# Copying the diagonal blocks of a recurrence on VectorE instead of GpSimd, with one step of the schedule cut from 1.7 to 1.25 chunks

## The chip, the cores and the metric

The kernel runs on one core of one Trainium2 chip. The metric is the device time in microseconds of one launch; lower is better. Short names of the engines: PE is TensorE, DVE is VectorE, ACT is ScalarE, POOL is GpSimd, SP is SyncE (it issues the weight loads).

## The reference, cut to what matters

Two layers; in each, one input projection feeds three branches (stick-breaking attention, latent attention, an RWKV-7 recurrence), and gates merge them. The change touches only the recurrence:

```python
def step(state, inp):
    r_t, w_t, k_t, v_t, a_t, b_t = inp
    sa = jnp.einsum('bhij,bhj->bhi', state, a_t)
    state = (state * w_t[:, :, None, :] + sa[..., None] * b_t[:, :, None, :]
             + v_t[..., None] * k_t[:, :, None, :])
    return state, jnp.einsum('bhij,bhj->bhi', state, r_t)
```

## The kernel before, in words

**Dense work.** Every weight matrix is streamed through SBUF as 280 chunks per layer (two blocks of 128 rows, mostly 512 columns). SP loads a chunk into a ring, ACT rounds it to its high half (`w_hi`, line 1043), DVE subtracts to get the low half (`w_lo`, the "split", line 1416), and PE multiplies: a chunk is 12 matmuls, six per half chunk (line 724). A split of a full chunk is a 128x1024 subtraction.

**Everything else is woven in by hand.** Each engine runs one program in a fixed order. The small work is divided into beats; `STEPS` gives each beat's length in chunks, and `beat_at(n)` turns the n-th beat into a position in the stream of chunks: the cumulated lengths are scaled so that all of them together fill the chunks 50 to 208, and each position is rounded down to half a chunk. PE runs to `beat_at(n)` in half chunks; DVE, ACT and POOL run to `int(beat_at(n))`. When DVE stands at position k it has split chunk k+2 (`LEAD` is 3), so PE, which waits for the count of splits at the first half of each chunk, can run at most through chunk k+2.

**The recurrence.** Eight heads are taken in four pairs of heads ("pair 0" to "pair 3"), 19 beats each, with two beats of other work between pair 0 and pair 1. A pair begins so:

- PE, after the pair's first beat: the score matmuls (16 of 64x256, line 829 through the helper at line 724), then `beat(4)`, that is four beats of dense work, then the first of four levels (`G1`, four small matmuls that need `WT`), a beat, `G2`, a beat, and so on.
- DVE: four predicated copies of 128x512 from PSUM put the masked scores into `AM` (line 1547); `beat(2)`; then, once POOL has copied the diagonal blocks, a chain of small operations that inverts the 8x8 blocks (lines 1551 to 1569, each linked to the one before, with one extra split at m == 2: `dense_to(int(beat_at(beats[0])) + 1)`); `beat()`; the tail of the chain (lines 1571 to 1583), whose transposes at line 1579 make `WT` and whose last product makes `WA`; `beat()`.
- POOL: four copies of 32x128, one per quarter of the partitions, take the diagonal blocks out of `AM` into `UC` (line 587), then the mask of the first level (line 575) and two copies (line 593).

For a pair whose first beat is number b+1, the score matmuls stand at `beat_at(b+1)`, the DVE chain after `beat_at(b+3)`, its tail after `beat_at(b+4)`, and `G1` of the first level at `beat_at(b+5)`. In the kernel before these positions are:

| pair | scores | after `beat(2)` | before the tail | `G1`, first level |
|---|---|---|---|---|
| 0 | 50.5 | 52.5 | 54.0 | 57.0 |
| 1 | 73.5 | 75.5 | 77.0 | 80.0 |
| 2 | 92.5 | 94.5 | 96.0 | 99.0 |
| 3 | 111.5 | 113.5 | 115.0 | 117.5 |

ACT evicts a finished group of dense columns from PSUM when it passes the group's last chunk (gates at 64, 72, 80, 88, ... 120, then `uq0` 122, `ukv0` 124, `uq1` 126, `ukv1` 128, and the recurrence's own gate `rg` at 144). For `rg` DVE has work too: it multiplies, transposes (lines 1462, 1416, 1446), all at its position 144. The latent attention's preparation for its second pair of heads (line 1641 a reduction, a beat, line 1644 a second one, a beat, line 1653 four scalings, a beat) stands around that point.

Of the kernel before, what the change touches and what calls it, by code (L numbers as in the profile page):

```python
# [59 lines left out]
LEVELS = 4  # L60
LEVELS_IN = 3
# [94 lines left out]
AT_KK = AT_Z + 1  # L156
AT_DECAY = AT_KK + 9
AT_PAIRS = AT_DECAY + 5
RW_STEPS = [1, 1.2, 1, 1.7, 2.96] + [0.92, 1.02] * LEVELS + [0.88] * 6
LATENT_STEPS = [2, 2.5]  # L160
GN_STEPS = [0.9] * 8
ML_PREP, ML_VISITS = [1.1, 1.2, 1.3, 1.2, 1.4, 1.4], [2, 1.5, 1.4]
# [2 lines left out]
SB_STEPS = [4, 3.5, 3]  # L165
RW_BEATS, GN_BEATS, ML_BEATS, SB_BEATS = len(RW_STEPS), len(GN_STEPS), len(ML_STEPS), len(SB_STEPS)
STEPS = RW_STEPS + LATENT_STEPS + 3 * RW_STEPS + GN_STEPS + ML_STEPS + SBH // 2 * SB_STEPS
AT_STEP = [sum(STEPS[:n]) for n in range(len(STEPS) + 1)]
# [27 lines left out]
AT_RW, AT_ML1, AT_SB = END["mg1"] + 2, END["mg1"] + 4, END["br0"]  # L196


RW_PE, RW_ACT, RW_DVE, RW_POOL = 8 + 2 * LEVELS, 5 + LEVELS, 5 + 2 * LEVELS, 6 + LEVELS_IN


def level_ready(n):

    if n >= LEVELS_IN:
        return RW_POOL - LEVELS + n
    return 5 if n == 1 else 6 + n


def program(nc, x, norm_g, w_in, mla_q_norm_g, mla_kv_norm_g, mla_w_uq, mla_w_ukv, mla_qn_g, mla_kn_g,
# [3 lines left out]
    with ExitStack() as ctx:  # L213
# [6 lines left out]
        def one(name):  # L220
            return ctx.enter_context(nc.semaphore(name))
# [30 lines left out]
        def units(n, u):  # L252
            return take(n).rearrange("p (u c) -> p u c", u=u)
# [21 lines left out]
        UC, WC = units(128, 4), units(128, 4)  # L275
# [3 lines left out]
        AM = units(2048, 4)  # L279
# [94 lines left out]
        rw_pe, rw_act, rw_dve, rw_pool = one("rw_pe"), one("rw_act"), one("rw_dve"), one("rw_levels")  # L374
# [145 lines left out]
        def _(pool):  # L520
# [7 lines left out]
            for l in range(DEPTH):  # L528
# [41 lines left out]
                def beat(count=1):  # L570
                    beats[0] += count
                    dense_to(int(beat_at(beats[0])))

                def rw_level(p, n):
                    nc.gpsimd.tensor_tensor(LM.rearrange("p u (a c) -> p u a c", a=2),
                                            UC.unsqueeze(2).to_broadcast([P, 4, 2, 32]),
                                            level[n].rearrange("p (a c) -> p a c", a=2).unsqueeze(1)
                                            .to_broadcast([P, 4, 2, 32]), ALU.mult).then_inc(rw_pool, 1)

                for p in range(4):  # L580
                    if p == 1:
                        beat(len(LATENT_STEPS))
                    beat()
                    pool.wait_ge(rw_dve, 4 * RW_DVE * l + RW_DVE * p + 2)
                    for q in range(4):
                        r = slice(32 * q, 32 * q + 32)
                        nc.gpsimd.tensor_copy(UC[r, :, :], AM[r, :, r]).then_inc(rw_pool, 1)  # L587
                    pool.wait_ge(rw_pool, 4 * RW_POOL * l + RW_POOL * p + 4)
                    rw_level(p, 1)
                    pool.wait_ge(rw_pool, 4 * RW_POOL * l + RW_POOL * p + 5)  # L590
                    for a in range(2):
                        r = slice(64 * a, 64 * a + 32)
                        nc.gpsimd.tensor_copy(LM5[r, :, 32 * a:32 * a + 32], AM[r, :, 64 * a + 32:64 * a + 64]
                                              ).then_inc(rw_pool, 1)
                    beat(4)
                    pool.wait_ge(rw_pool, 4 * RW_POOL * l + RW_POOL * p + 7)
                    for n in range(1, LEVELS_IN - 1):
                        pool.wait_ge(rw_pe, 4 * RW_PE * l + RW_PE * p + 1 + 2 * n)
                        rw_level(p, n + 1)
                        beat(2)  # L600
                    pool.wait_ge(rw_pe, 4 * RW_PE * l + RW_PE * p + 2 * LEVELS_IN - 1)
                    nc.gpsimd.tensor_copy(LM, AM[:, :, 64:128]).then_inc(rw_pool, 1)
                    pool.wait_ge(rw_pool, 4 * RW_POOL * l + RW_POOL * p + RW_POOL)
                    if p < 3:
                        turned = OPS_TURN.rearrange("p h (i j t) -> p h i j t", i=4, j=4)
                        moved = TT2[(p + 1) % 2].rearrange("p h (i j t) -> p h i j t", i=4, j=4)
                        pool.wait_ge(ops_turned, 3 * l + p + 1)
                        for d in range(4):
                            for i in range(4):
                                j = (i + d) % 4  # L610
                                nc.gpsimd.tensor_copy(moved[32 * j:32 * j + 32, :, :, i, :],
                                                      turned[32 * i:32 * i + 32, :, :, j, :]).then_inc(quarters, 1)
                            pool.wait_ge(quarters, 16 * (3 * l + p) + 4 * d + 4)
                        pool.sem_inc(ops_moved, 1)
                    beat(6)
                    beat(6)
# [49 lines left out]
                for q in range(SBH // 2):  # L666
# [6 lines left out]
                    for e in range(2):  # L673
                        pool.wait_ge(sb_act, 8 * l + 4 * q + 3 + e)
                        for c0 in (0, 256):
                            part = AZ[e][:, c0:c0 + P]
                            last = nc.gpsimd.affine_select(out=part, in_=part, compare_op=ALU.is_gt, fill=0.0,
                                                           base=0, pattern=[[1, P]], channel_multiplier=-1)
# [41 lines left out]
        def _(pe):  # L720
# [26 lines left out]
            def dense_to(end):  # L747

                while at[0] < end:
                    n, kk = int(at[0]), round(at[0] % 1 * KC)  # L750
                    gi, c = CHUNKS[n]
                    name, _, _, cols, blocks = GROUPS[gi]
                    if kk == 0:
                        if c == 0 and gi >= 2:
# [284 lines left out]
        def _(act):  # L1039
# [27 lines left out]
            def take_out(end):  # L1067
                while group[0] < len(GROUPS) and END[GROUPS[group[0]][0]] <= end:
                    gi = group[0]
                    name, _, _, cols, blocks = GROUPS[gi]  # L1070
                    group[0] += 1
                    kind, no = name.rstrip("0123456789"), int(name[-1]) if name[-1].isdigit() else 0
# [332 lines left out]
        def _(dve):  # L1405
            v = nc.vector
            at, group, beats, order = [0], [GI["rg"]], [0], [0]

            def link(ins):

                order[0] += 1
                ins.then_inc(dve_seq, 1)
                dve.wait_ge(dve_seq, order[0])

            def tt(o, a, b, op):
                return v.tensor_tensor(o, a, b, op)  # L1416
# [18 lines left out]
            def beat(count=1):  # L1435
                for _ in range(count):
                    beats[0] += 1
                    dense_to(int(beat_at(beats[0])))
# [95 lines left out]
            def rw_pair(p):  # L1534
# [10 lines left out]
                    dve.wait_ge(rw_pool, 4 * RW_POOL * l + RW_POOL * p)  # L1545
                for u in range(4):
                    last = v.copy_predicated(AM[:, u, :], con[:, K_RWM:K_RWM + 512].bitcast(U32), B[u][:])  # L1547
                last.then_inc(rw_dve, 1)
                beat(2)
                dve.wait_ge(rw_pool, 4 * RW_POOL * l + RW_POOL * p + 4)  # L1550
                blocks = own_block.unsqueeze(1).unsqueeze(3).to_broadcast([P, 4, 32 // EDGE, EDGE])
                wide = WIDE[:, 0:128].rearrange("p (u j c) -> p u j c", u=4, j=32 // EDGE)
                link(tt(wide, UC.rearrange("p u (j c) -> p u j c", c=EDGE), blocks, ALU.mult))
# [7 lines left out]
                for m in range(1, EDGE - 1):  # L1561
                    n, c0 = EDGE - 1 - m, 32 - m
# [15 lines left out]
                for g in range(2):  # L1578
                    last = v.transpose(WT[64 * g:64 * g + 64, :, 32 * g:32 * g + 32], WC[64 * g:64 * g + 64, :, :])  # L1579
# [5 lines left out]
                for n in range(1, LEVELS_IN):  # L1585
                    beat()
                    dve.wait_ge(rw_pe, 4 * RW_PE * l + e + 2 * n + 2)
                    for g, (odd, rows) in product(range(2), PARITY):
                        half = slice(32 * g, 32 * g + 32)
                        t = WT[64 * g:64 * g + 64, odd, half]  # L1590
                        last = tt(t, t, G2[rows:rows + 64, odd, half], ALU.add)
                    last.then_inc(rw_dve, 1)
                    dve.wait_ge(rw_dve, 4 * RW_DVE * l + RW_DVE * p + 2 * n + 3)
                    for q in (1, 3) if n == LEVELS_IN - 1 else range(4):
                        r = slice(32 * q, 32 * q + 32)
                        last = v.transpose(WA[r, :, q % 2 * 32:q % 2 * 32 + 32], WT[r, :, q // 2 * 32:q // 2 * 32 + 32])
                    last.then_inc(rw_dve, 1)
                    if p < 3:
                        if n == 1 and p:
                            dve.wait_ge(ops_moved, 3 * l + p)  # L1600
                        for i in (2 * n - 2, 2 * n - 1):
                            s = (KK, R[:, :, 0:512], AA, R[:, :, 512:1024])[i]
                            last = v.transpose(OPS_TURN[:, :, i * P:(i + 1) * P], s[:, :, (p + 1) * P:(p + 2) * P])
                        if n == LEVELS_IN - 1:
                            last.then_inc(ops_turned, 1)
                    if n == LEVELS_IN - 1:
                        for q in range(4):
                            r = slice(32 * q, 32 * q + 32)
# [4 lines left out]
                for odd, rows in PARITY:  # L1613
                    last = v.transpose(WT6[32:64, odd, 0:32], G2[rows:rows + 32, odd, 0:32])
                last.then_inc(rw_dve, 1)
                for i, (odd, rows) in product(range(2), PARITY):
                    r = rows + 32 * i
                    last = v.tensor_copy(WF[64 * i:64 * i + 32, odd, 64 * i + 32:64 * i + 64], G2[r:r + 32, odd, 0:32])
# [3 lines left out]
                for odd, rows in PARITY:  # L1622
                    last = v.tensor_copy(WF[0:64, odd, 64:128], G2[rows:rows + 64, odd, :])
# [149 lines left out]
            for l in range(DEPTH):  # L1773
# [47 lines left out]
                for h in range(HALVES):  # L1821
                    last = v.scalar_tensor_tensor(S1[:, h, :], AA[:, h, :], -1.0, ROWS[:, 512:1024], ALU.add, ALU.mult)
                link(last)
                dense_to(AT_KK + 2)
                for h in range(HALVES):
                    last = v.scalar_tensor_tensor(R[:, h, 512:1024], S1[:, h, :], 1.0, R[:, h, 512:1024],
                                                  ALU.add, ALU.mult)
# [20 lines left out]
                for h in range(HALVES):  # L1848
                    last = v.scalar_tensor_tensor(KK[:, h, :], KK[:, h, :], -1.0, S3[:, h, :], ALU.mult, ALU.mult)
# [10 lines left out]
                for p in range(4):  # L1860
                    if p == 1:
                        latents()
                    rw_pair(p)
# [90 lines left out]
```

## Time and profile before

| | |
|---|---|
| runs | 1682.27, 1680.42, 1680.75 us; median 1680.75 us |
| profiled execution, its own time | 1682.79 us |
| its span, first to last instruction | 1681.0 us |
| PE busy / DVE / ACT / POOL | 1665.9 / 1154.5 / 841.7 / 489.8 us |
| TensorE clock granted | 1.00 of full speed throughout (the 2.4 GHz level) |
| HBM | 195 GB/s over the span |

How to read it: matmuls are pipelined and their ends are modelled, so "busy" of PE includes waits shorter than about the 0.16 us by which a matmul's shown 0.39 us exceeds the spacing of two matmuls. Waits of PE are therefore read here as distances between starts. In a timeline a row is start, duration, engine, line, operation, the tiles, the shapes, the count of merged instructions, and in brackets the idle time before it and who ended it. Lines are those of the kernel before.

### The profile page before, as it was taken

How to read it: one execution, taken by the hardware profiler on the slowest of the kernel's cores; microseconds unless marked ns; L12 is line 12 of the kernel's file. 1: busy time of each engine (PE TensorE's matmuls, PEld its weight loads, DVE VectorE, ACT ScalarE, POOL GpSimd, SP SyncE). 2: the span in 40 equal slices, each digit the busy share in tenths (PEclk: the TensorE clock that was granted, in tenths of full speed). 3: DMA queues.
4: the chain of work that ended last, by engine and by line, in shares of the span. 5: the costliest groups of instructions: out<-in, count | busy, mean ns of one | idle time of the engine just before them, and what ended most of it. 6: DMA issues, size and time to landing. Idle time of an engine off the chain costs nothing.

```text
span 1681.0 us, 21448 instructions
## 1 busy us (share of the span) xinstructions
PE 1665.9 (99%) x8010; PEld 1390.0 (83%) x8010; DVE 1154.5 (69%) x1667; ACT 841.7 (50%) x1221; POOL 489.8 (29%) x722
## 2 busy tenths in 40 slices
PE   7999999999999999999999999999999999999999
PEld 6878888888888888888888788888888888888887
DVE  4668775866976566886656786857778665578853
ACT  6544554435545455555454445534445544555542
POOL 1011313410343426362400112233103534245500
PEclk9999999999999999999999999999999999999999
DMA  8865656656665557785687656556566565668764
GB/s 260 262 179 184 185 166 189 183 159 189 180 183 172 176 163 235 234 307 188 207 264 229 180 175 178 187 163 200 162 180 181 168 177 177 187 211 289 262 193 158
DMA packets 176912, 332.72 MB, mean 198 GB/s; under 512 B 19516, under 2 KB 32746, under 8 KB 176808
## 3 DMA queue, kind: packets, MB, share of 16 engines
q1 hardware_dynamic: 167048, 297.86, 58.3%
q0 software_dynamic: 9584, 33.42, 5.7%
q8 instruction: 63, 1.03, 0.3%
q14 instruction: 41, 0.34, 0.1%
q10 hardware_dynamic: 176, 0.07, 0.0%
HBM read 311.14 MB, written 16.78 MB: 195 GB/s over the span
## 4 chain that ended last, share of the span: by engine, by line
PE 90%; DVE 4%; ACT 2%; DMA 1%; SPq 1%; issue 1%; POOL 1%; ACTq 0%; DVEq 0%
PE D L724 81%; PE B L724 8%; DMA ring<-in_w_in 1%; DVE w_lo L1416 1%; DVE arena L1416 1%; ACT w_hi L1043 1%; POOL arena L587 1%; ACT arena L1043 1%; DVE arena L1547 0%; PE B L915 0%; DVE xy L1416 0%; SPq L464 0%; ACT gev L1043 0%; PE B L894 0%; DVE ht_lo L1750 0%
## 5 line engine op out<-in xcount | busy, mean ns | idle before, releaser
L1416 DVE TENSOR_TENSOR w_lo<-ring,w_hi 128x1024 fp32r<-128x1024 f32 (+3 forms) x560 | 677.1, 1223 | 330.8 <-ACT w_hi L1043 321.9
L1043 ACT ACTIVATE w_hi<-ring 128x1024 fp32r<-128x1024 f32 (+3 forms) x560 | 575.0, 1038 | 486.1 <-PE D L724 379.4
L724 PE MATMUL D<-w_hi,ht_hi 128*128 128x512 f32 (+2 forms) x1728 | 680.7, 394 | 4.3 <-DVE w_lo L1416 4.1
L724 PE MATMUL D<-w_hi,ht_lo 128*128 128x512 f32 (+2 forms) x1728 | 665.5, 385 | 0.0
L724 PE MATMUL D<-w_lo,ht_hi 128*128 128x512 f32 (+2 forms) x1728 | 664.8, 385 | 0.0
L724 PEld LDWEIGHTS D<-w_hi,ht_hi 128*128 128x128 f32 x1728 | 325.0, 188 | 74.1 <-issue 8.8
L724 PEld LDWEIGHTS D<-w_hi,ht_lo 128*128 128x128 f32 x1728 | 324.6, 188 | 65.9
L724 PEld LDWEIGHTS D<-w_lo,ht_hi 128*128 128x128 f32 x1728 | 325.2, 188 | 58.9 <-issue 0.5
L626 POOL COPY arena<-arena 32x256 f32<-32x256 f32 x240 | 163.2, 680 | 144.6 <-DVE arena L1446 108.9
L724 PEld LDWEIGHTS B<-arena 128*128 128x128 f32 (+2 forms) x928 | 121.7, 190 | 20.8 <-issue 8.1
L1043 ACT ACTIVATE arena<-B 64x64 f32<-64x64 f32 (+6 forms) x186 | 54.9, 300 | 165.0 <-PE B L724 158.8
L643 POOL COPY arena<-arena 32x384 f32<-32x384 f32 x128 | 95.8, 748 | 135.3 <-PE B L724 103.1
L724 PE MATMUL B<-arena 128*128 128x128 f32 (+4 forms) x928 | 132.7, 295 | 1.7 <-DVE arena L1579 0.7
L724 PE MATMUL D<-w_hi,mt_lo 128*128 128x512 f32 x256 | 100.5, 392 | 0.0
L724 PE MATMUL D<-w_hi,mt_hi 128*128 128x512 f32 x256 | 100.3, 392 | 0.0
L724 PE MATMUL D<-w_lo,mt_hi 128*128 128x512 f32 x256 | 100.0, 390 | 0.0
L566 POOL DMA_DIRECT2D gate_spill<-gev x24 | 17.8, 742 | 251.9 <-ACT gev L1043 250.8
L1416 DVE TENSOR_TENSOR arena<-arena 128x1024 f32<-128x1024 f32 (+9 forms) x168 | 86.4, 514 | 5.1 <-DMA arena<-arena 0.3
L587 POOL COPY arena<-arena 32x128 f32<-32x128 f32 x32 | 24.0, 749 | 166.6 <-DVE arena L1547 165.2
L1043 ACT ACTIVATE arena<-arena 128x1024 f32<-128x1024 f32 (+5 forms) x88 | 58.9, 669 | 11.4 <-DVE arena L1416 7.8
L1043 ACT ACTIVATE gev<-D,small 128x512 f32<-128x512 f32 (+1 forms) x64 | 40.4, 680 | 35.5 <-PE D L724 35.3
L724 PEld LDWEIGHTS D<-w_lo,mt_hi 128*128 128x128 f32 x256 | 48.1, 188 | 10.7
(163 smaller groups left out, 1386.8 us busy)
## 6 DMA issues: line engine op xcount, KB each, us to landing
ring<-in_w_in SPq DMA_DIRECT2D x368, 512.0 KB, 4.5
ring<-in_w_out SPq DMA_DIRECT2D x64, 512.0 KB, 5.2
ring<-in_w_br_mla SPq DMA_DIRECT2D x32, 512.0 KB, 5.5
gate_spill<-gev POOLq DMA_DIRECT2D x24, 512.0 KB, 4.7
arena<-gate_spill POOLq DMA_DIRECT2D x24, 512.0 KB, 5.7
ring<-in_mla_w_ukv SPq DMA_DIRECT2D x16, 512.0 KB, 4.4
ring<-in_w_br_rw SPq DMA_DIRECT2D x16, 512.0 KB, 5.2
ring<-in_w_br_sb SPq DMA_DIRECT2D x16, 512.0 KB, 5.4
```

Source lines behind the costliest of these rows:

```text
L566: pool.dma_start(spill[n].rearrange("(h p) c -> p h c", p=P), gev[:, n % 2, :, :]).then_inc(spilled[n % 2][l], 16)
L587: nc.gpsimd.tensor_copy(UC[r, :, :], AM[r, :, r]).then_inc(rw_pool, 1)
L626: nc.gpsimd.tensor_copy(moved[32 * j:32 * j + 32, :, :, i, :], turned[32 * i:32 * i + 32, :, :, j, :]).then_inc(quadrants[l], 1)
L643: nc.gpsimd.tensor_copy(moved[32 * j:32 * j + 32, :, i, :], turned[32 * i:32 * i + 32, :, j, :]).then_inc(ml_quarters, 1)
L724: return nc.tensor.matmul(o, a, b, start=start, stop=stop, skip_group_check=True)
L1043: return nc.scalar.activation(o, i, fn, **kw)
L1416: return v.tensor_tensor(o, a, b, op)
```

## The change

DVE makes the four 32x128 copies right behind its predicated copies, linked to the last of them; POOL no longer makes them and starts with the first level's mask. POOL's count of signals per pair drops by four. DVE's later wait is on its own copies. The length of the step behind the masked scores is 1.25 instead of 1.7 chunks for each of the four pairs of each layer; since all lengths are scaled to the same 158 chunks, every other step grows by 1%, and positions move by up to one chunk.

```diff
-RW_STEPS = [1, 1.2, 1, 1.7, 2.96] + [0.92, 1.02] * LEVELS + [0.88] * 6
+RW_STEPS = [1, 1.2, 1, 1.25, 2.96] + [0.92, 1.02] * LEVELS + [0.88] * 6
...
-RW_PE, RW_ACT, RW_DVE, RW_POOL = 8 + 2 * LEVELS, 5 + LEVELS, 5 + 2 * LEVELS, 6 + LEVELS_IN
+RW_PE, RW_ACT, RW_DVE, RW_POOL = 8 + 2 * LEVELS, 5 + LEVELS, 5 + 2 * LEVELS, 2 + LEVELS_IN
...
-    return 5 if n == 1 else 6 + n
+    return 1 if n == 1 else 2 + n
...
                     pool.wait_ge(rw_dve, 4 * RW_DVE * l + RW_DVE * p + 2)
-                    for q in range(4):
-                        r = slice(32 * q, 32 * q + 32)
-                        nc.gpsimd.tensor_copy(UC[r, :, :], AM[r, :, r]).then_inc(rw_pool, 1)
-                    pool.wait_ge(rw_pool, 4 * RW_POOL * l + RW_POOL * p + 4)
                     rw_level(p, 1)
-                    pool.wait_ge(rw_pool, 4 * RW_POOL * l + RW_POOL * p + 5)
+                    pool.wait_ge(rw_pool, 4 * RW_POOL * l + RW_POOL * p + 1)
...
                     last = v.copy_predicated(AM[:, u, :], con[:, K_RWM:K_RWM + 512].bitcast(U32), B[u][:])
+                link(last)
+                for q in range(4):
+                    r = slice(32 * q, 32 * q + 32)
+                    last = v.tensor_copy(UC[r, :, :], AM[r, :, r])
                 last.then_inc(rw_dve, 1)
                 beat(2)
-                dve.wait_ge(rw_pool, 4 * RW_POOL * l + RW_POOL * p + 4)
+                dve.wait_ge(rw_dve, 4 * RW_DVE * l + RW_DVE * p + 2)
```

## Rows read from the trace of the kernel before

**Rows 1.** The page, busy time of an engine, its share and instructions:

```profile
PE 1665.9 (99%) x8010; PEld 1390.0 (83%) x8010; DVE 1154.5 (69%) x1667; ACT 841.7 (50%) x1221; POOL 489.8 (29%) x722
```

**Rows 2.** Waits: engine, line, releaser, us in total, times, longest:

```profile
DVE arena L1416 <- POOL arena L587: 7.4, 8, 1.2
```

**Rows 3.** Timeline of DVE, layer 0, pair 1:

```profile
229.42 2.61 DVE L1547 COPY_PREDICATED arena<-con,B 128x512 f32<-128x512 uint32 x4 [2.54 <-PE B L724]
231.92 2.44 DVE L1416 TENSOR_TENSOR w_lo<-ring,w_hi 128x1024 fp32r<-128x1024 f32 x2
235.24 0.29 DVE L1416 TENSOR_TENSOR arena<-arena,con 128x128 f32<-128x128 f32 x1 [0.88 <-POOL arena L587]
...
242.78 1.22 DVE L1416 TENSOR_TENSOR w_lo<-ring,w_hi 128x1024 fp32r<-128x1024 f32 x1
243.93 0.65 DVE L1416 TENSOR_TENSOR arena<-arena,con 128x256 f32<-128x256 f32 x1
...
245.40 0.62 DVE L1579 STREAM_TRANSPOSE arena<-arena 64x128 f32<-64x128 f32 x2
...
246.40 3.49 DVE L1416 TENSOR_TENSOR w_lo<-ring,w_hi 128x1024 fp32r<-128x1024 f32 x3
```

**Rows 4.** Timeline of PE, layer 0, pair 1:

```profile
229.31 0.50 PE L724 MATMUL D<-w_hi,ht_hi 128*128 128x512 f32 x1
...
244.44 0.39 PE L724 MATMUL D<-w_hi,ht_hi 128*128 128x512 f32 x1
...
245.80 0.39 PE L724 MATMUL D<-w_hi,ht_hi 128*128 128x512 f32 x1
...
247.16 0.61 PE L724 MATMUL B<-arena 128*128 128x128 f32 x4
247.76 0.47 PE L724 MATMUL D<-w_hi,ht_hi 128*128 128x512 f32 x1
...
249.56 0.68 PE L724 MATMUL B<-arena 128*128 128x128 f32 x4 [0.17 <-ACT arena L1043]
```

**Rows 5.** Timeline of PE, layer 0, pair 3:

```profile
354.87 0.50 PE L724 MATMUL D<-w_hi,ht_hi 128*128 128x512 f32 x1
...
371.88 0.71 PE L724 MATMUL B<-arena 128*128 128x128 f32 x4 [0.34 <-DVE arena L1579]
...
381.28 0.61 PE L724 MATMUL B<-arena 128*128 128x128 f32 x4
...
383.28 0.71 PE L724 MATMUL B<-arena 128*128 128x128 f32 x4 [0.32 <-DVE arena L1416]
...
392.31 0.61 PE L724 MATMUL B<-arena 128*128 128x128 f32 x4
392.68 0.42 PE L724 MATMUL D<-w_hi,cq_hi 128*128 128x384 f32 x1
...
393.81 0.55 PE L724 MATMUL B<-arena 128*128 128x64 f32 x4
```

**Rows 6.** Timeline of ACT, layer 0, pair 1 at the first level:

```profile
247.36 1.27 ACT L1043 ACTIVATE gev<-D,small 128x512 f32<-128x512 f32 x2 [1.60 <-PE D L724]
```

**Rows 7.** One line's instructions (ns min/median/max), the nearest copy in SBUF:

```profile
L1845 DVE COPY arena<-arena x2: 226/226/227, 133.6 to 965.1; 128x128 f32<-128x128 f32 x2
```

**Rows 8.** Timeline of POOL, layer 0, pair 1:

```profile
232.10 3.10 POOL L587 COPY arena<-arena 32x128 f32<-32x128 f32 x4 [6.40 <-DVE arena L1547]
235.29 0.84 POOL L575 TENSOR_TENSOR arena<-arena,con 128x256 f32<-128x256 f32 x1
```

**Rows 9.** Timeline of DVE, layer 0, behind the gate at chunk 144:

```profile
454.92 0.64 DVE L1644 TENSOR_REDUCE small<-arena 128x4 f32<-128x512 f32 x1
...
455.70 1.21 DVE L1416 TENSOR_TENSOR w_lo<-ring,w_hi 128x1024 fp32r<-128x1024 f32 x1
456.84 1.64 DVE L1653 SCALAR_TENSOR_TENSOR arena<-arena,small 128x192 f32<-128x192 f32 x4
```

**Rows 10.** Timeline of PE, layer 0, the same place, chunk 147:

```profile
456.97 0.50 PE L724 MATMUL D<-w_hi,ht_hi 128*128 128x512 f32 x1 [0.43 <-DVE w_lo L1416]
```

More of the change, by code:

```diff
@@ L595, in _ @@
                     beat(4)
-                    pool.wait_ge(rw_pool, 4 * RW_POOL * l + RW_POOL * p + 7)
+                    pool.wait_ge(rw_pool, 4 * RW_POOL * l + RW_POOL * p + 3)
                     for n in range(1, LEVELS_IN - 1):
```

## The prediction

> **What bounds the kernel now.** I read the page's busy times first: PE is busy 99% of the span [rows 1], so no work elsewhere counts unless PE waits for it. Then the table of waits: DVE waited for POOL's diagonal copies eight times, once per pair and layer, for 7.4 us in all [rows 2]; the largest thing the change can take away is therefore idle time of an engine that is not the bound. Then the timelines of PE and DVE side by side, pair by pair, because the busy share hides short waits: there the distances between starts are compared. They show that PE does lose time in the recurrence, in small pieces. All times below are in pair 1's clock of layer 0; pair 0 repeats it 75 us earlier, and layer 1 repeats layer 0.
>
> **What PE loses before.** Twelve matmuls from 244.44 to 247.16 [rows 4] give 0.227 us each. The first level's `G1` of pair 1 is followed by dense work after 0.60 us [rows 4], where a `G1` without a wait takes 0.37 [rows 5]: 0.24, because the split of the next chunk, the first of the three at 246.40 [rows 3], ends only then. Pair 0 does the same. The half chunk behind it takes 1.80 us to `G2` [rows 4], six matmuls being 1.36 plus about 0.1 at the restart: about 0.35, as ACT was evicting a gate, 1.27 us from 247.36 [rows 6], before it could copy `G1`'s result. Pair 3 needs 17.01 us for the 72 matmuls from 354.87 to 371.88 [rows 5], which pair 1 does from 229.31 to 245.80, 16.49 us [rows 4]: 0.52, and about 0.1 within the `G1` that waits for line 1579. At its third level the way from `G2` to `G1` takes 2.00 us, against 1.50 for the same six narrower matmuls later [rows 5]: 0.5 and another 0.1. The sum is 0.48 + 0.35 + 0.62 + 0.6 = 2.05 per layer, with a tenth or two in pairs 0 and 2 about 2.4: **4.8 us in two layers is all that the change can win.** By the same reading of starts the rest of the program has little to give.
>
> **The copies.** DVE's predicated copies run from 229.42 to 232.03, the two splits behind them start at 231.92, and the chain starts at 235.24 after 0.88 us of waiting for POOL [rows 3]. After: a link (about 0.03), four copies, then the same two splits, then the chain without a wait. The nearest copy in SBUF with 128 elements per partition took 0.226 us [rows 7], four of them 0.90; with a gap I take 0.92. The splits then start about 1.0 to 1.1 us later than before, and the 0.88 us goes: **the chain starts 0.12 us later, not earlier.** The wait was hidden behind the splits, and the copies are not. Bounds, as estimates around that row: 0.17 each (a quarter under it, for a quarter of its partitions) to 0.30 (a third over it, for a strided source), so the chain starts between 0.1 earlier and 0.45 later.
>
> A rule speaks here: the Trainium skill, VectorE: DVE Perf Modes, section "The TRN2 errata — SBUF-src ops pay a fixed extra latency per instruction", gives 58 cycles plus elements over the mode's speed-up at 0.96 GHz, that is an estimated 0.13 us for 128 elements at double speed, but notes that a fixed term near 150 cycles was measured, which gives 0.22. The row's 0.226 us agrees with the second [rows 7]; by the first the copies would cost 0.4 us less per pair, and the time would come out about 3.3 us lower, at 1683.3 us.
>
> **The step.** The lengths sum to 172.7 instead of 174.5, scaled to the same 158 chunks. Rounded down to half chunks, the positions after are:
>
> | pair | scores | after `beat(2)` | before the tail | `G1` |
> |---|---|---|---|---|
> | 0 | 50.5 | 52.5 | 54.0 | 56.5 |
> | 1 | 73.5 | 75.5 | 76.5 | 79.5 |
> | 2 | 92.0 | 94.0 | 95.5 | 98.0 |
> | 3 | 111.0 | 113.0 | 114.0 | 117.0 |
>
> Between scores and `G1` PE now has 6.0 chunks in every pair (6.5, 6.5, 6.5, 6.0 before). DVE takes the integer part, and m == 2 already takes it one chunk past `beat(2)`: in pairs 1 to 3 the step before the tail brings no split any more (76, 95, 114 are reached at m == 2), so `WT` comes 243.93 - 242.78 = 1.15 us earlier [rows 3] less the 0.12, and that split now follows the tail. What PE may do before the tail is over is chunk k+2.
>
> - Pair 0 keeps its split at 54. `WT` is ready at 245.40 + 0.62 + 0.12, with a handoff of 0.06 at 246.20; PE arrives half a chunk earlier, at 245.80 [rows 3, 4]. New wait **0.45**; the wait behind `G1` goes.
> - Pair 1: DVE stands at 76 and PE may run through chunk 78, but `G1` stands at 79.5 and needs the first half of chunk 79. PE asks for it at 244.44 [rows 4]. Its split, which ended just before that in the kernel before (242.78 + 1.22 [rows 3]), now follows the tail: the tail and `WA` take 246.40 - 243.93 = 2.47 us [rows 3], so the split starts at 242.78 + 0.12 + 2.47 = 245.37, ends at 246.59, and PE goes on some 0.14 later, as it did after the first of the three splits before. New wait **2.3**. Behind PE's wait for this chunk stand `G1`, and so ACT's copy and DVE's next additions. The half chunk before `G2` stays, but the gate's eviction moves behind ACT's copy, so that 0.35 goes.
> - Pairs 2 and 3: DVE stands at 95 and 114, enough for exactly the six chunks. `G1` starts at 245.80 without waiting, but the next dense chunk, asked for 0.37 later, waits for the first split behind the tail until 246.73: **0.57** each. The losses of pair 3 named above go.
> - In pair 3 the gate of chunk 120 is now evicted between `G2` of the second and `G1` of the third level, with narrow chunks behind it. ACT's 1.27 us [rows 6] comes ahead of two small copies that `G2` needs; I put **0.3**, between nothing and 0.5.
>
> New waits per layer: 0.45 + 2.3 + 0.57 + 0.57 + 0.3 = 4.2, or 8.4 in all, for the 4.8 that go.
>
> **Behind the recurrence** the latent attention stands up to a chunk earlier. At the gate `rg` (chunk 144) DVE's position 144 moves one beat back, behind line 1644, and position 145 behind line 1653. PE asked for chunk 147 just when its split ended: it waited 0.43 [rows 10] for the split at 455.70 [rows 9]. After, the scalings of line 1653 (1.64 us [rows 9]) stand ahead of that split and the reduction of line 1644 with its addition (0.78, from 454.92 to 455.70 [rows 9]) no longer: 0.8 later, and some 0.3 because ACT's work on the first squares now delays its sigmoids. **1.1 per layer**, 2.2 in all, bounds 0 and 1.6 each.
>
> **Sum.** 8.4 + 2.2 - 4.8 = +5.8 us on the profiled execution's span of 1681.0 (its own time is 1682.79, some 2 us above the median, of which 1.79 lie outside the span and are not touched). On the median: 1680.75 + 5.8, **1686.5 us**.
>
> **Rivals.**
> 1. *Not slower: the copies cost nothing.* If DVE stands idle before the splits anyhow (waiting for ACT's high half), the copies fill that time and the chain starts 0.88 earlier. Then pair 0, 2 and 3 have no new wait and pair 1 has 1.3: with 0.3 that is 3.2 in two layers, less 4.8, and with the gate's order harmless 1679.2 us. It decides when the chain starts 0.6 or more earlier. Against it: 231.92 follows 232.03 without a gap [rows 3]. For it: that row is pair 1's, and another pair's splits may wait for ACT.
> 2. *Within the bound: only the recurrence changes.* The gate at 144 and ACT at 120 cost nothing: 1680.75 + 7.8 - 4.8 = 1683.7 us. For it: the 0.43 there is one layer's [rows 10], the order of three engines decides it, and I have no row of the new order.
> 3. *Worse: POOL gets in ahead of the splits.* POOL's first mask, 0.84 us [rows 8], is now released by the same event behind which the splits start. Before, POOL's four copies took 3.10 us because the splits were ahead of them [rows 8]; if POOL starts first and the split is held until it is done, every pair's chain is 0.84 later: 4 x 0.84 x 2 = 6.7, 1693.2 us. Against it: the splits need no signal, POOL does. The Trainium skill, SBUF — State Buffer, section "SBUF: two separate sides", states that the pair of ports shared by the two engines is locked for a whole instruction by whoever starts first; POOL's 3.10 us agrees with that, in the order DVE first.
>
> **Chances.** Forecast 0.73, rival 1 0.07, rival 2 0.15, rival 3 0.05. A difference of 0.2%, 3.4 us, is about what a measurement of this kernel tells from none. Slower (above 1684.1): the forecast less the part of its bounds below that, and rival 3, 0.76. Within: rival 2, most of rival 1 and that part, 0.20. Faster: 0.04, since even all 4.8 us without any new wait would be only 0.29%. Range: the copies' bounds move four waits in two layers by -1.9 to +2.4, the gate -2.2 to +1.0, ACT -0.6 to +0.4; 1682.5 to 1690.0 holds 8 in 10.
>
> **What would show it.** Right: PE waits about 2 us for a `w_lo` split in pair 1 of both layers ahead of `G1`, the largest wait in the table of PE; DVE's wait for POOL is gone, yet its chain starts about 5.9 us after the first predicated copy instead of 5.8 [rows 3]; pair 3's waits for lines 1579 and 1416 are gone. Wrong: no wait of PE over 1 us in pair 1 (then the order of split and tail is not as I read it), a chain that starts over 0.5 us earlier, or copies of more than 0.3 us each. The gate at 144 shows in PE's wait for chunk 147, 1 to 2 us.

## The result, and the profile after

The changed kernel takes **1693.49 us**, median of 5 runs (1691.10 to 1696.42), against 1680.75: a ratio of 1.0075, 95% interval 1.0063 to 1.0086. It is slower, as forecast, but by 12.7 us where 5.8 were forecast, and outside the range of 1682.5 to 1690.0.

Its profiled execution took 1691.10 us with a span of 1689.3, 8.3 more than before's. The page, busy time of an engine, its share and instructions (answers [rows 1]):

```profile
PE 1666.2 (99%) x8010; PEld 1389.6 (82%) x8010; DVE 1165.1 (69%) x1699; ACT 843.4 (50%) x1221; POOL 477.7 (28%) x690
```

PE does the same work in the same busy time; the 8.3 us are waits. The table of waits for PE (engine, line, releaser, total us, times, longest); the row of [rows 2], DVE waiting for POOL, has no counterpart any more:

```profile
PE D L720 <- DVE w_lo L1412: 12.5, 15, 2.6
```

The timeline of DVE in pair 1 of layer 0 (answers [rows 3]; lines 589 to 1543 of the kernel after are 593 to 1547 of before, and each experiment's lines are its own kernel's):

```profile
228.17 2.60 DVE L1543 COPY_PREDICATED arena<-con,B 128x512 f32<-128x512 uint32 x4 [2.54 <-PE B L720]
230.80 0.91 DVE L1547 COPY arena<-arena 32x128 f32<-32x128 f32 x4
231.74 2.91 DVE L1412 TENSOR_TENSOR w_lo<-ring,w_hi 128x1024 fp32r<-128x1024 f32 x2
234.58 0.37 DVE L1412 TENSOR_TENSOR arena<-arena,con 128x128 f32<-128x128 f32 x1
...
243.68 0.62 DVE L1579 STREAM_TRANSPOSE arena<-arena 64x128 f32<-64x128 f32 x2
...
244.68 3.49 DVE L1412 TENSOR_TENSOR w_lo<-ring,w_hi 128x1024 fp32r<-128x1024 f32 x3
```

The same from 233.3 us on, which leaves the second of the two splits alone in its row:

```profile
232.89 1.77 DVE L1412 TENSOR_TENSOR w_lo<-ring,w_hi 128x1024 fp32r<-128x1024 f32 x1
```

And POOL's timeline there (answers [rows 8]):

```profile
231.80 1.77 POOL L575 TENSOR_TENSOR arena<-arena,con 128x256 f32<-128x256 f32 x1 [7.36 <-DVE arena L1547]
233.63 1.51 POOL L589 COPY arena<-arena 32x128 f32<-32x128 f32 x2
```

The copies cost what was forecast, 0.91 us. But the two splits behind them take 2.91 us instead of 2.44: the first runs its usual time, the second 1.77 us instead of 1.2. POOL's mask starts with the first split, lasts 1.77 us instead of 0.84, and ends 0.68 us after the second split began. So the chain starts 6.41 us after the first predicated copy (228.17 to 234.58), where before's took 5.82: **0.59 later instead of 0.12**. Between the chain and its tail no split stands any more, and three follow the tail at 244.68.

In pair 3 the chain is as late (6.39 us after the first predicated copy), but there another wait decides. ACT evicts a gate ahead of the high half that the second split needs (ACT's and DVE's timelines of pair 3):

```profile
358.49 1.27 ACT L1039 ACTIVATE gev<-D,small 128x512 f32<-128x512 f32 x2 [3.80 <-PE D L720]
```

```profile
359.07 1.23 DVE L1412 TENSOR_TENSOR w_lo<-ring,w_hi 128x1024 fp32r<-128x1024 f32 x1
360.74 1.24 DVE L1412 TENSOR_TENSOR w_lo<-ring,w_hi 128x1024 fp32r<-128x1024 f32 x1 [0.44 <-ACT w_hi L1039]
```

PE's timeline in layer 0: pair 1 (answers [rows 4]), pair 2, pair 3 (answers [rows 5]), and the gate (answers [rows 10]):

```profile
242.96 0.39 PE L720 MATMUL D<-w_hi,ht_lo 128*128 128x512 f32 x1
245.95 0.50 PE L720 MATMUL D<-w_hi,ht_hi 128*128 128x512 f32 x1 [2.61 <-DVE w_lo L1412]
...
308.46 0.61 PE L720 MATMUL B<-arena 128*128 128x128 f32 x4
309.87 0.50 PE L720 MATMUL D<-w_hi,ht_hi 128*128 128x512 f32 x1 [0.81 <-DVE w_lo L1412]
...
371.89 0.60 PE L720 MATMUL B<-arena 128*128 128x128 f32 x4
373.30 0.50 PE L720 MATMUL D<-w_hi,ht_hi 128*128 128x512 f32 x1 [0.80 <-DVE w_lo L1412]
...
385.93 0.63 PE L720 MATMUL B<-arena 128*128 128x64 f32 x4 [0.16 <-ACT arena L1039]
...
460.14 0.50 PE L720 MATMUL D<-w_hi,ht_hi 128*128 128x512 f32 x1 [1.01 <-DVE w_lo L1412]
```

By distances between starts, as in the prediction: pair 1 loses 2.99 - 0.23 = 2.77 us, pairs 2 and 3 1.41 - 0.37 = 1.05 each, pair 0 0.46 and 0.47 for two waits of 0.29, pair 3's ACT copies 0.33. That is 6.1 per layer. At the gate the wait grows from 0.43 [rows 10] to 1.01; layer 1, where before's trace shows no such wait, loses 1.17. Together 12.2 + 0.6 + 1.2 = 14.0 us of new waits.

What went in return can be read as well, since PE runs the same 6722 matmuls of dense work in the same order in both kernels. The start of the same one in both:

| the same dense matmul | before | after | later by |
|---|---|---|---|
| layer 0, ahead of pair 0's first level | 159.17 | 157.07 | -2.10 |
| layer 0, behind the four pairs | 449.57 | 452.16 | 2.59 |
| layer 0, behind the gate | 678.28 | 681.48 | 3.20 |
| layer 1, ahead of pair 0's first level | 997.44 | 1000.41 | 2.97 |
| layer 1, behind the four pairs | 1283.11 | 1290.58 | 7.47 |
| layer 1, behind the gate | 1514.75 | 1523.07 | 8.32 |

The four pairs cost 4.7 and 4.5 us net and the gates 0.6 and 0.85: **10.7 us**. So of the 12.2 us of new waits in the pairs only 3.0 were won back. Profile to profile it is 8.3, since before's profiled execution is 2.1 us behind ahead of the first pair, in the opening, where the change alters nothing.

The other four runs of the kernel after lie 2.1 to 5.3 us above the profiled one, with a mean granted clock of 0.998 or 0.999 where the profiled one has 1.000. This profile can't show what took them; the experiments do.

### The profile page after: what moved, and what is told of

Same layout as the page of the kernel before. It is cut to its first block, busy times and chain, and to the rows that moved or that the text cites. A ratio compares the mean times of both kernels' runs of the same rounds, so it can differ in the third digit from the quotient of the medians.

```text
span 1689.3 us, 21442 instructions
## 1 busy us (share of the span) xinstructions
PE 1666.2 (99%) x8010; PEld 1389.6 (82%) x8010; DVE 1165.1 (69%) x1699; ACT 843.4 (50%) x1221; POOL 477.7 (28%) x690
## 4 chain that ended last, share of the span: by engine, by line
PE 85%; DVE 9%; ACT 2%; DMA 1%; issue 1%; SPq 1%; ACTq 0%; DVEq 0%
PE D L720 76%; PE B L720 8%; DVE w_lo L1412 3%; DVE arena L1412 3%; DMA ring<-in_w_in 1%; DVE arena L1543 1%; ACT w_hi L1039 1%; ACT arena L1039 0%; ACT gev L1039 0%; DVE xy L1412 0%; DVE arena L1547 0%; PE B L911 0%; DVE arena L1579 0%; DVE gev L1458 0%; SPq L449 0%
## 5 line engine op out<-in xcount | busy, mean ns | idle before, releaser
L720 PE MATMUL D<-w_hi,ht_hi 128*128 128x512 f32 (+2 forms) x1728 | 681.0, 394 | 12.7 <-DVE w_lo L1412 12.5
L622 POOL COPY arena<-arena 32x256 f32<-32x256 f32 x240 | 167.5, 698 | 143.6 <-DVE arena L1442 107.9
L639 POOL COPY arena<-arena 32x384 f32<-32x384 f32 x128 | 90.4, 707 | 134.1 <-PE B L720 83.8
L575 POOL TENSOR_TENSOR arena<-arena,con 128x256 f32<-128x256 f32 x16 | 22.9, 1430 | 249.4 <-DVE arena L1547 174.5
L720 PEld LDWEIGHTS D<-w_hi,mt_lo 128*128 128x128 f32 x256 | 48.1, 188 | 11.2
```

What stands on the lines that cost most here:

```text
L639: nc.gpsimd.tensor_copy(moved[32 * j:32 * j + 32, :, i, :], turned[32 * i:32 * i + 32, :, j, :]).then_inc(ml_quarters, 1)
L720: return nc.tensor.matmul(o, a, b, start=start, stop=stop, skip_group_check=True)
```

## The experiments

Each time is a median, beside runs of before on the same chip, with medians of 1681.0 to 1681.3; the intervals are of the ratio to before, and the clocks are each run's mean.

**The two parts apart.** First the copies on DVE with the step back at 1.7:

```diff
-RW_STEPS = [1, 1.2, 1, 1.25, 2.96] + ...
+RW_STEPS = [1, 1.2, 1, 1.7, 2.96] + ...
```

> After, with the step behind the masked scores back at 1.7 chunks: the copies on VectorE alone. Late-split theory (most of the loss comes from TensorE coming sooner than the split that stands behind the chain): no wait near 2.7 us in pair 1; the chain starts 0.6 us later than in before because the two splits beside POOL's mask still take 2.9 us, which adds at most 0.6 us to each of the waits that before has in pairs 1 and 3 and as much at new places, 1 to 2 us a layer: 1682.5 to 1685, granted clock 1.000 in every run. Rival (the copies on VectorE with the contention beside them are the cause): 1689 to 1693.

Measured 1685.64 us, 1.0028 (1.0017 to 1.0038), clock 1.000 in all 8 runs. So the copies alone cost 4.5 us, just above what the theory gave. The chain starts 6.41 us after the first predicated copy here too, and in layer 0 PE loses 0.3 to 0.6 us by starts at nine places from the first pair to the gate, where before's profile has four.

Then before with the step at 1.25, POOL still copying (the same edit the other way):

> Before, with the step behind the masked scores at 1.25 chunks: POOL still copies the blocks. Late-split theory: the chain starts 5.8 us after the first predicated copy, as in before, and the waits of after stay less 0.6 us each: pair 1 about 2.2 us, pairs 2 and 3 about 0.45, pair 0 next to nothing, the gate 1.2: 2.5 us a layer less than after's profiled 1691.1, so 1686, up to 1688 if the clock falls in some executions as it does in after. Rival (the copies are the cause): 1680.5 to 1682.

Measured 1691.64 us, 1.0060 (1.0047 to 1.0073), the clock 0.998 or 0.999 in all 5 runs. The waits came near the forecast (1.95 us in pair 1, 0.25 in pair 2, 1.19 at the gate), but for pair 3 (0.88 instead of 0.45); the time is above what they give. In pair 3 the second split waits for ACT's high half here too, and longer, so that the chain starts 6.70 us after the first predicated copy:

```profile
358.98 1.55 DVE L1416 TENSOR_TENSOR w_lo<-ring,w_hi 128x1024 fp32r<-128x1024 f32 x1 [1.54 <-ACT w_hi L1043]
```

**The step is the larger part.** Together the parts cost 12.7 us where they add up to 15, but the intervals leave room for an equal sum.

This profile caught the clock. The table by stretches in pair 1 of layer 1 (stretch, us, busy time of PE, PEld, DVE, ACT, POOL, granted clock, DMA share, GB/s), and PE's timeline:

```profile
1078.00:1080.00 2.00, 0.11 (x1) 0.11 (x1) 1.97 (x4) 0.00 (x0) 0.00 (x0) 1.00 0.01 4
1080.00:1081.00 1.00, 1.00 (x4) 0.80 (x5) 1.00 (x2) 0.00 (x0) 0.00 (x0) 0.71 0.14 16
1081.00:1082.00 1.00, 1.00 (x4) 0.81 (x3) 1.00 (x1) 0.00 (x0) 0.00 (x0) 0.50 0.82 188
1082.00:1083.00 1.00, 1.00 (x6) 0.91 (x5) 0.11 (x1) 0.00 (x0) 0.00 (x0) 0.50 0.95 344
1083.00:1084.00 1.00, 1.00 (x5) 0.83 (x4) 0.00 (x0) 0.68 (x4) 0.60 (x1) 0.59 0.86 252
1084.00:1085.00 1.00, 1.00 (x7) 0.82 (x6) 0.00 (x0) 0.97 (x2) 0.13 (x1) 1.00 1.05 385
```

```profile
1077.58 0.39 PE L724 MATMUL D<-w_hi,ht_lo 128*128 128x512 f32 x1
1079.89 0.50 PE L724 MATMUL D<-w_hi,ht_hi 128*128 128x512 f32 x1 [1.93 <-DVE w_lo L1416]
...
1080.91 0.63 PE L724 MATMUL D<-w_hi,ht_hi 128*128 128x512 f32 x1
1081.34 0.63 PE L724 MATMUL D<-w_lo,ht_hi 128*128 128x512 f32 x1
```

PE waited 1.93 us for the late split, ran for half a microsecond, and was then granted 0.50, the 1.2 GHz level, until nearly 1084: matmuls start every 0.43 us instead of 0.23. The granted shares of the four stretches add to 2.30 us out of 4, so one fall costs **1.7 us**. In layer 0 of the same execution a wait of 1.95 us passed without it.

**One split later, and nothing else.** Before, with its copies and its step, but the split of chunk 79 in pair 1 behind the tail:

```diff
                 link(v.transpose(INVERSE[:, 0:EDGE - 1, :], INVERSE_T))
-                beat()
+                if p == 1:
+                    beats[0] += 1
+                else:
+                    beat()
```

> Before, with one split moved: in pair 1 the split of chunk 79, which stands ahead of the last products of the chain, is issued behind the tail, as the shorter step makes it; the copies stay on POOL and the step at 1.7. Late-split theory: TensorE waits 1.8 us for it (the split would end at 246.45 where TensorE is ready for it at 244.67) and the waits of 0.17 us behind it go: 1.5 us a layer, 1684 in a profile. If a wait of this length is what lowers the clock, the mean clock is 0.999 in most runs, a run loses 1.7 us for each layer in which it falls, and the median is 1685 to 1687. Rival (the clock falls for something else that the step or the copies bring): 1.000 in all runs and 1684.

Measured 1686.79 us, 1.0033 (1.0022 to 1.0043). PE's timeline in pair 1 of the profiled execution, which is one of two with the clock at 1.000:

```profile
242.54 0.39 PE L724 MATMUL D<-w_hi,ht_lo 128*128 128x512 f32 x1
244.85 0.50 PE L724 MATMUL D<-w_hi,ht_hi 128*128 128x512 f32 x1 [1.92 <-DVE w_lo L1416]
```

The wait is there (1.92). The two runs at 1.000 took 1684.75 and 1685.02 us; the six at 0.998 or 0.999 took 1685.69 to 1689.23. Neither the copies nor the step is needed for the loss of clock: the one split that comes late brings it in most runs.

**One split earlier.** After, with that split put ahead of the chain's last transpose:

```diff
+                if p == 1:
+                    dense_to(int(beat_at(beats[0])) + 2)
                 link(v.transpose(INVERSE[:, 0:EDGE - 1, :], INVERSE_T))
```

> After, with one split of pair 1 taken from behind the chain and its tail and put ahead of the chain's last transpose. Late-split theory: TensorE no longer waits 2.7 us for chunk 79; it goes on to the first product behind the chain, 1.4 us further, which now comes 1.2 us later and makes it wait about 1.2: 1.5 us a layer less, 1688 in a profile. If the long wait is what lowers the clock in four of five runs of after, the clock is 1.000 in all runs and the median is 1688 too, 5.5 us below after's 1693.5; if the clock falls for another cause, it falls here too and the median is about 1690.5. Rival (the split's place does not matter, VectorE is late with everything): the same as after.

Measured 1689.99 us, 1.0049 (1.0036 to 1.0061), clock 1.000 in all 5 runs. `G1` now waits 0.76 for the tail (1.2 was expected), and 3.5 us of after's time are gone, where 5.5 were expected; the runs lie between 1688.79 and 1690.26. The clock came out as expected; what the rest is, these runs don't show.

The same on the kernel with the step alone:

> The step at 1.25 with the copies on POOL, and one split of pair 1 taken from behind the chain and put ahead of the chain's last transpose, as was done to after. Late-split theory: the wait of 1.95 us in pair 1 becomes one of 0.3 us for the tail, the clock is 1.000 in every run, and what stays of the step's price are the waits of pairs 2 and 3 and the gate: 1685 to 1686.5, against 1691.6 for the step alone. Rival (the shorter step costs by itself): 1690 or more.

Measured 1685.58 us, 1.0024 (1.0015 to 1.0033), clock 1.000 in all 11 runs: 6.1 us less than the step alone, as forecast. The largest waits left in its profile are those of pair 3 (0.88), the gate (1.20) and pair 2 (0.23).

**POOL's mask beside the splits.** After, with the mask held until both splits are done:

```diff
                     pool.wait_ge(rw_dve, 4 * RW_DVE * l + RW_DVE * p + 2)
+                    pool.wait_ge(split_lo, l * NCH + int(beat_at(beats[0] + 2)))
```

> After, with POOL's first mask held until VectorE's two splits behind the copies are done. Contention theory: the two splits take 2.44 us again and the chain starts 0.47 us sooner; the waits of pairs 0 to 3 shrink by that each, two of them in pair 0: 2.3 us a layer, 1686.4 in a profile; the pair 1 wait is still 2.3 us, so that the clock may fall as before and the median lie up to 2.4 higher. Rival (the splits are slow because they follow the copies, whatever POOL does): 2.9 us still, and the time of after.

Measured 1691.17 us, 1.0058 (1.0045 to 1.0070), clock 0.998 or 0.999 in all 5 runs. DVE's and POOL's timelines of pair 1:

```profile
230.74 2.36 DVE L1413 TENSOR_TENSOR w_lo<-ring,w_hi 128x1024 fp32r<-128x1024 f32 x2
233.02 0.29 DVE L1413 TENSOR_TENSOR arena<-arena,con 128x128 f32<-128x128 f32 x1
233.34 0.39 DVE L1555 TENSOR_REDUCE arena<-arena 128x32 f32<-128x128 f32 x1
233.77 0.84 DVE L1413 TENSOR_TENSOR arena<-arena,con 128x224 f32<-128x224 f32 x1
```

```profile
233.63 0.73 POOL L575 TENSOR_TENSOR arena<-arena,con 128x256 f32<-128x256 f32 x1 [10.18 <-DVE w_lo L1413]
```

The splits are back at 2.36 us, so that POOL's mask is what slowed them here. But the median fell by 2.3 us in all, where 2.3 per layer had been expected. In pair 3 the wait for ACT stayed (0.43) and the chain starts 6.36 us after the first predicated copy, as in after. In the other pairs the mask now starts 0.14 us ahead of a product of the chain, and that takes 0.84 us instead of 0.39. The cost had moved by a few instructions. The clock fell here as well, in layer 1 behind a wait of 2.04 us, and not in layer 0 behind one of 2.40.

So the mask was made smaller instead, with the copies on DVE and the step at 1.7 (at the first level it masks block 0 of the four alone, and the kernel leaves the other three out):

> The copies on VectorE with the step at 1.7, as in the run of the copies alone, but POOL's first mask of each pair works on one of the four blocks only, so that the other three of that operand are left as they were. What is left of the copies' price without most of the mask beside the splits. Contention theory: the two splits take close to 2.44 us, the chain starts 5.9 to 6.0 us after the first predicated copy (before 5.82, copies alone 6.41), and the time is 1681 to 1682.5. Rival (the copies cost by themselves, in VectorE's own order): the time of the copies alone, 1685.5.

Measured 1681.95 us, 1.0006 (0.9997 to 1.0015), clock 1.000 in all 11 runs. DVE's and POOL's timelines of pair 1:

```profile
228.25 2.60 DVE L1546 COPY_PREDICATED arena<-con,B 128x512 f32<-128x512 uint32 x4 [2.54 <-PE B L723]
230.88 0.91 DVE L1550 COPY arena<-arena 32x128 f32<-32x128 f32 x4
231.83 2.49 DVE L1415 TENSOR_TENSOR w_lo<-ring,w_hi 128x1024 fp32r<-128x1024 f32 x2
234.24 0.37 DVE L1415 TENSOR_TENSOR arena<-arena,con 128x128 f32<-128x128 f32 x1
```

```profile
231.89 1.35 POOL L585 TENSOR_TENSOR arena<-arena,con 128x64 f32<-128x64 f32 x1 [7.36 <-DVE arena L1550]
```

The chain starts 5.99 us after the first predicated copy, and 3.7 of the 4.5 us that the copies cost are gone. What stays, 0.9 us, is not clear of nothing (by the interval -0.5 to 2.5): **at this step the copies themselves cost little, and what they let POOL do costs the rest.**

**Both causes out of after**, the early split and the small mask together:

> After, with both causes taken out at once: the split of pair 1 is put ahead of the chain's last transpose, and POOL's first mask of each pair works on one of the four blocks only, so that the other three of that operand are left as they were. If the late split with its clock and the mask beside the splits are all that after has over the other waits of the shorter step, the time is that of the step with the early split, 1685.6, and 0.9 for the copies themselves, 1686.5, at a clock of 1.000. Rival (the two parts of the change have a further cost together): 1688.5 or more.

Measured 1688.49 us, 1.0036 (1.0022 to 1.0050). The interval reaches from 1685.0 to 1689.7 us and holds both answers. Two of the five runs took 1685.51 and 1686.50. The profiled one, the slowest, has waits in the recurrence near those of the step with the early split (0.40 in pair 2, 0.77 in pair 3, 1.19 at the gate), but also waited 1.86 us for a split in the opening, at 33 us, and behind that the clock fell and matmuls started every 0.43 us.

By the starts of the same dense matmuls, from ahead of the first pair to behind the second gate, this profile loses 5.4 us against before's, and the step with the early split 4.5. The difference is the 0.9 us of the copies, as expected; between these two profiles the opening, which no edit alters, makes 3.9 us. So the profile shows no further cost of the two parts together. Why two more runs, at a clock of 1.000, took some 1688.5 stays open.

**Looking for a version that beats before.** A step of 1.8 instead of 1.7 on before:

> Before, with the step at 1.8 chunks instead of 1.7, the other direction: the first product behind the chain then stands half a chunk later in pair 3 and the one after it half a chunk later in pairs 0, 1 and 2. Late-split theory: the waits of 0.3 us in pair 3 for the tail and of 0.2 in pair 1 go and no split comes later, 0.8 us a layer, 1679.5. Rival (a longer step only lengthens the chain): 1681 to 1683.

Measured 1681.62 us, 1.0002 (0.9993 to 1.0010): no change, where 1679.5 was expected. The waits of pairs 1 and 3 did go, but the profile has a new one of 0.29 us in each layer behind the recurrence, at 636 and 1467 us, which before's has not. Two copies on each engine, step 1.7:

> Before (step 1.7), with two of the four blocks copied on VectorE and two on POOL. VectorE pays 0.46 us ahead of the two splits; POOL's two copies take 1.55 us beside them and are done before them, so that the wait of 0.88 us for POOL goes. The chain starts 0.4 us sooner if POOL's mask behind the copies does not slow the second split, and as in before if it does (0.45 us): 1679.5 to 1681. If sooner chains are worth nothing: 1681.

Measured 1685.21 us, 1.0022 (1.0013 to 1.0031); the clock was 0.999 in one of 11 runs. POOL's two copies, and the chain's first product:

```profile
231.00 2.57 POOL L587 COPY arena<-arena 32x128 f32<-32x128 f32 x2 [6.88 <-DVE arena L1551]
```

```profile
233.68 0.86 DVE L1416 TENSOR_TENSOR arena<-arena,con 128x128 f32<-128x128 f32 x1 [0.26 <-POOL arena L587]
```

Two copies of POOL's take 2.57 us beside the splits, not 1.55 as expected, so that a wait of 0.26 stays; and the mask meets the first product, which takes 0.86 us instead of 0.29. The four copies on ACT, step 1.7:

```diff
                     act.sem_inc(rw_act, 1)
-                beat(5)
+                beat()
+                dense_to(int(beat_at(beats[0])) + 1)
+                act.wait_ge(rw_dve, 4 * RW_DVE * l + RW_DVE * p + 2)
+                for q in range(4):
+                    r = slice(32 * q, 32 * q + 32)
+                    last = f(UC[r, :, :], AM[r, :, r])
+                last.then_inc(rw_act, 1)
+                beat(4)
```

> After's structure with the step at 1.7 and the four copies on ScalarE, in a gap of 1.66 us between two of its evictions of weights; VectorE goes straight on with its two splits. At 0.31 us each the copies take 1.25 us and end before the first split does, so that POOL's mask then runs beside the second split and costs it 0.45 us: the chain starts 0.4 us sooner than in before, and the waits of 0.3 us in pair 3 and 0.2 in pair 1 shrink: 1679 to 1680.5. If ScalarE is late with its own next eviction, the waits come back there: 1681 to 1683.

Measured 1684.61 us, 1.0019 (1.0010 to 1.0028). DVE's timeline:

```profile
234.62 1.23 DVE L1419 TENSOR_TENSOR w_lo<-ring,w_hi 128x1024 fp32r<-128x1024 f32 x1 [1.32 <-ACT w_hi L1039]
```

The copies took 1.27 us on ACT, but stood ahead of its next eviction of weights, and DVE's second split waited 1.32 us for that. No version beat before.

## Why the prediction was right in sign and wrong in size

- *What PE loses before, and can win back.* Right as to the kinds: the waits of pair 3 for lines 1579 and 1416, of pair 1 for ACT, and DVE's for POOL are gone. But they were sized too large: 3.0 us were won back in the pairs, not 4.8. A part of that is the restart behind a wait, some 0.1 us (245.95 to 246.28 in the new code, where two matmuls stand 0.23 apart): the forecast counted it in what goes and not in what comes.
- *The copies' duration.* Right: 0.91 us against 0.92.
- ***The start of the chain: this step failed.*** "0.12 later" left out what else the event that frees POOL sets going. Before, POOL's mask came when the splits were over; after, it is released by the last copy and gets in between the two. It was rival 3, at a chance of 0.05, with the order wrong (POOL first) and 0.84 us as its price; measured 0.47 a chain, 2.91 against 2.44. With it the new waits are 6.1 us per layer instead of 4.2, that is 3.8 more in all. At the step of 1.7 the run with the copies alone and the one with the small mask show the mask's price: 3.7 us. In after the mask does it in pairs 0 to 2; in pair 3, where the scores come half a chunk sooner, the second split waits 0.44 us for ACT, a wait that rival 1 had named as possible, though to save time and not to cost it. That rival 3's 1693.2 us lies next to the measured 1693.49 is luck: its 6.7 us stand for 3.8, and for the clock and the waits not won back, which it did not have.
- *The rule that was weighed against that rival.* The Trainium skill, SBUF — State Buffer, section "SBUF: two separate sides", has the pair of ports that POOL shares with a DVE operation of two SBUF inputs locked for a whole instruction by whoever starts first. The rows agree, and for both orders: the mask waits out the first split, and the second split waits out the mask (1.77 us each); in the run with the mask held, the product that came 0.14 us behind the mask's start ended 0.45 late. The rule was cited against the rival because DVE came first; it says nothing of who gets the ports between two instructions of one engine, and here it was the other engine.
- *The order of split and tail.* Right: pair 1's wait was 2.77 where 2.3 were forecast, the largest in PE's table; pairs 2 and 3 1.05 (0.57), pair 0 0.93 (0.45, where its own figures give 0.40), the differences being the later chain; ACT 0.33 (0.3). Moving that one split moved the time in the direction that the theory said each time, and with after by less than it said (3.5 of 5.5).
- *The gate.* Somewhat less: 0.6 and 1.2 of new waits in the two layers, 0.6 and 0.85 net, against 1.1 each.
- ***The clock: a term that was missing.*** A long wait of PE was priced at its length. It also brings, in most executions, a fall of the granted clock right behind it, 1.7 us each time. After's median lies 2.4 us above its profiled run, which had none.
- *The sum and its base.* In the terms of the forecast, 5.8 and 3.8 for the later chains and 1.8 for what was not won back, less 0.7 at the gates, make the 10.7 that the profiles show; one or two falls of the clock bring it to between 12.4 and 14.1, against the 12.7 of the medians. Before's profiled run lies 2.0 us above its median; its opening is 2.1 us longer than after's, with a wait for a split of 1.38 us where after's has one of 0.30.

Rivals 1 and 2 are out: no chain starts earlier with all four copies on DVE, and the gates did cost.

## What to carry to other kernels

Before moving work away from an idle engine, ask what that engine does next and beside what it will then run; here that cost 3.7 us, and the moved work itself 0.9, which is not clear of nothing. When positions of a schedule are rounded down, list for each place which weight preparation falls behind a serial chain and what the consumer needs by then: one split that slipped behind the chain cost 5.8 us by itself, more than the whole gain in sight. Price a wait of the matrix engine of some 2 us above its length, and look at each run's mean clock, since a single profile may not hold the fall. Compare two profiles stretch by stretch, by the starts of the same instructions: among the profiles of this case the opening alone, which no edit alters, differs by up to 3.9 us.

## What the runs showed of the hardware

- The granted clock fell to 0.50 behind waits of PE of 1.93 and 2.04 us in the recurrence and of 1.86 us in the opening, each time 0.3 to 0.5 us after PE had resumed, and for 3.4 us; it stayed at 1.00 behind others of 1.91 to 2.61 us. Which of them brings a fall stays open. Over the runs, 20 of 23 of the four kernels with such a wait in pair 1 show a mean below 1.000, and 1 of 68 of the seven changed kernels without one, the kernel with both causes out left aside; of the 72 runs of before beside them it is 1.
- A POOL operation beside two splits of DVE took far longer than elsewhere: a quarter of the mask 1.35 us and the whole 1.77, the whole behind the splits 0.73 to 0.84; two copies 2.57, and two like them in before, behind the splits, 0.68. What the splits lost goes with the operation: the two took 2.36 us with POOL idle, 2.44 to 2.45 beside copies, 2.49 beside a quarter of the mask and 2.91 beside the whole.
